# Norm chains of a two-block transformer kernel: filler products in PE's waits, a rounding without its lag, and earlier halves of two activation splits

## What is computed

```python
def modulate(x, shift, scale):
    return layer_norm(x) * (1 + scale) + shift
...
def mixer(p, kv, lw, rope):
    ...
    g_f, g_m, g_g = jnp.split(jax.nn.sigmoid(gate_logits + lw["b_gate"]), N_BRANCHES, axis=-1)
    return (g_f * y_f + g_m * y_m + g_g * y_g) @ lw["w_o"]

def sq_relu_mlp(h, lw):
    return jnp.square(jax.nn.relu(h @ lw["w1"])) @ lw["w2"]
...
        h_x = modulate(x, sh1, sc1)
        p_x = h_x @ lw["w_in"]
...
        x = layer_norm(alpha * x + g1 * mix_x, ln1_g[l], ln1_b[l])
        x = layer_norm(alpha * x + g2 * sq_relu_mlp(modulate(x, sh2, sc2), lw), ln2_g[l], ln2_b[l])
```

## Time and profile before

| | |
|---|---|
| median of 3 runs | 3077.68 us (3077.47 to 3078.82) |
| the profiled execution: its own time | 3078.22 us |
| its span, first to last instruction | 3076.0 us |
| mean granted TensorE clock | 0.959 of full speed |
| PE busy | 2901.8 us, 94% of the span |
| ACT, DVE, POOL busy | 1264.1, 963.1, 1813.2 us |

### The profile page before, as it was taken

How to read it: one execution, slowest core, us unless ns; L and a number is a source line. 1 busy time by engine, 2 the same in 40 slices (tenths; PEclk the granted TensorE clock), 3 DMA queues, 4 the chain that set the end, 5 groups by cost and what they waited for, 6 DMA issues and landing times.

```text
span 3076.0 us, 49253 instructions
## 1 busy us (share of the span) xinstructions
PE 2901.8 (94%) x20337; PEld 2573.1 (84%) x20337; DVE 963.1 (31%) x1757; ACT 1264.1 (41%) x1675; POOL 1813.2 (59%) x1380
## 2 busy tenths in 40 slices
PE   6989889999999998898999998999999999899999
PEld 4866658757878686797998998989999999889999
DVE  3133233232122334434144314144321314144331
ACT  2323533223222243644444435454444434455443
POOL 1310217414455240485895997747898997856896
PEclk8989989989999899998998999999999999999999
DMA  7325333212322234453553555534555556534553
GB/s 228 90 94 170 115 123 111 87 55 92 99 83 96 69 84 131 146 175 110 177 195 111 185 179 147 162 95 152 177 178 171 185 178 153 165 110 136 170 188 124
DMA packets 397419, 422.61 MB, mean 137 GB/s; under 512 B 74577, under 2 KB 367433, under 8 KB 396957
## 3 DMA queue, kind: packets, MB, share of 16 engines
q1 hardware_dynamic: 397246, 420.11, 44.1%
HBM read 419.01 MB, written 3.16 MB: 137 GB/s over the span
## 4 chain that ended last, share of the span: by engine, by line
PE 84%; POOL 5%; DVE 4%; ACT 2%; issue 2%; DMA 1%; SPq 1%; DVEq 0%; POOLq 0%; ACTq 0%
PE ps L830 64%; PE ps L814 18%; POOL ring_r L1637 5%; PE ps L857 2%; ACT ring_hi L1670 1%; DMA ring<-in_w_in 0%; DVE stat L2595 0%; SPq L596 0%; DVE arena_r L2818 0%; PE ps L1315 0%; DVE arena L2609 0%; DVE arena L2874 0%; SPq L562 0%; DVE arena L2568 0%; DMA ring<-in_ffn_w_up 0%
## 5 line engine op out<-in xcount | busy, mean ns | idle before, releaser
L1637 POOL TENSOR_TENSOR ring_r<-ring,ring_hi 128x512 fp32r<-128x512 f32 x1376 | 1813.0, 1355 | 1240.3 <-ACT ring_hi L1670 1239.9
L830 PE MATMUL ps<-hT_r,ring_hi 128*128 128x256 f32 (+1 forms) x6176 | 1148.2, 309 | 37.9 <-POOL ring_r L1637 23.8
L830 PEld LDWEIGHTS ps<-hT_r,ring_hi 128*128 128x128 f32 x6176 | 927.4, 195 | 111.5 <-issue 47.2
L1670 ACT ACTIVATE ring_hi<-ring 128x2048 fp32r<-128x2048 f32 x344 | 655.3, 1911 | 379.6 <-DMA ring<-in_ffn_w_down 110.3
L830 PE MATMUL ps<-hT_r,ring_r 128*128 128x256 f32 (+1 forms) x3088 | 695.7, 307 | 0.0
L830 PE MATMUL ps<-arena_r,ring_hi 128*128 128x256 f32 (+1 forms) x3536 | 598.7, 311 | 24.3 <-DVE arena_r L2684 10.1
L830 PEld LDWEIGHTS ps<-arena_r,ring_hi 128*128 128x128 f32 x3536 | 509.7, 193 | 63.6 <-issue 20.2
L830 PEld LDWEIGHTS ps<-hT_r,ring_r 128*128 128x128 f32 x3088 | 510.0, 195 | 24.2
L830 PE MATMUL ps<-arena_r,ring_r 128*128 128x256 f32 (+1 forms) x1768 | 334.4, 308 | 0.0
L830 PEld LDWEIGHTS ps<-arena_r,ring_r 128*128 128x128 f32 x1768 | 267.4, 192 | 16.1
L814 PE MATMUL ps<-arena 128*64 128x128 f32 (+9 forms) x1616 | 198.6, 362 | 26.3 <-DVE arena L2572 11.9
(11 more groups left out here) (295 smaller groups left out, 2376.0 us busy)
## 6 DMA issues: line engine op xcount, KB each, us to landing
ring<-in_w_in SPq DMA_DIRECT2D x82, 1024.0 KB
ring<-in_w SPq DMA_DIRECT2D x64, 1024.0 KB
ring<-in_w_ada SPq DMA_DIRECT2D x48, 1024.0 KB
ring<-in_ffn_w_up SPq DMA_DIRECT2D x44, 1024.0 KB
ring<-in_ffn_w_gate SPq DMA_DIRECT2D x44, 1024.0 KB
ring<-in_ffn_w_down SPq DMA_DIRECT2D x44, 1024.0 KB
ring<-in_w_in SPq DMA_DIRECT2D x48, 256.0 KB
ring<-in_w_o SPq DMA_DIRECT2D x8, 1024.0 KB
```

Source lines behind the costliest of these rows:

```text
L830: last[t] = pe.matmul(o, lhsT, rhs, start=start and j == 0, stop=stop and j == n - 1, skip_group_check=True)
L1637: ins = pool.tensor_tensor(k.ring_lo[s][:, part], k.ring[s][:, part], k.ring_hi[s][:, part], ALU.subtract)
L1670: act.activation(k.ring_hi[s][:, :], k.ring[s][:, :], ACT.Copy).then_inc(k.hi_ready[s], 1)
```

## The change

It makes five edits, all in the first block.

1. `awake(b, n)` issues n products of the identity with 256 columns of constants (plain float32, 128x128x256) into a bank that is about to be written anyway. In each of the four norm chains one stands before the statistics products, and four (two in the last chain) before the flip; nine stand before the first norm's panel.
2. In `coefficients` the `ends` flips move ahead of part 0, and part 1 behind the product with ones. Part 4 moves from before the first tile of h to after it.
3. `modulate_tokens` rounds each tile right behind its own L1715. DVE's low half follows two steps back instead of three. Where this norm is followed by two panels, one of ACT's `split` calls moves in behind tile 4, and is taken out further on.
4. The first half of the split of `mixed` (four tiles) moves into the last branch group: ACT's two roundings behind its sigmoids there, DVE's two subtractions ahead of its last four gated tiles.
5. The last round of up panels is unrolled. Hidden tiles 0 and 1 are rounded and subtracted ahead of the last two tiles' rectifying and squaring, and PE takes the down products of tile 0 bank by bank, each as its bank comes free.

```diff
+            def awake(b, n):
+
+                for _ in range(n):
+                    pe.matmul(ps[:, b, 0:256], ident, k.const[:, 0:256], start=True, stop=True, skip_group_check=True)
...
                 b = bank()
+                awake(b, 1)
                 pe.wait_ge(*k.moved(sums))
...
                 b = bank()
+                awake(b, 4 if tiles else 2)
                 pe.wait_ge(S["rows_ready"], T.next("rows_ready"))
...
-                part(0)
                 b = bank()
                 pe.wait_ge(S["rows_ready"], T.next("rows_ready"))
...
-                part(1)
+                part(0)
                 pe.wait_ge(*k.moved(ends))
                 T.again(b)
                 products(ps[:, b, 0:n], [(ones[0:1, :], token_ends[0:1, 0:n])]).then_inc(k.bank_done[b], 1)
+                part(1)
                 part(2)
...
                 part(3)
-                part(4)
                 w = view(panel(), 0, KD, 256)
                 for kt in range(KD):
-                    if 1 <= kt <= 3:
-                        part(kt + 4)
+                    if 1 <= kt <= 4:
+                        part(kt + 3)
...
+                    bs = [bank() for _ in range(2)]
+                    awake(bs[0], 9)
                     w = view(panel(), 0, KD, 256)
-                    bs = [bank() for _ in range(2)]
...
-                        bs = [bank() for _ in range(KD)]
-                        done = [(b, T.value(f"bank{b}")) for b in bs]
-                    mms = abreast([ps[:, b, 0:n] for b in bs],
-                                  [[(cut(w, ALL, kt % 2, slice(m * P, m * P + P)), x)] for m in range(KD)], kt == 0, False)
+                        bs, done, mms = [], [], []
+                        for m in range(KD):
+                            bs.append(bank())
+                            done.append(T.last())
+                            mms.append(products(ps[:, bs[m], 0:n], [(cut(w, ALL, 0, slice(m * P, m * P + P)), x)], True, False))
...
-                for kt in range(KD + 1):
...
+                    ins.then_inc(S["h_plain"], 1)
+                    act.wait_ge(S["h_plain"], T.next("h_plain"))
+                    act.activation(k.h[0][:, kt, cols], plain[:, kt, cols], ACT.Copy).then_inc(S["h_rounded"], 1)
+                    if kt == KD // 2 and last:
+                        split()
...
+                        if (c, g) == (1, 2):
+                            mixed_half(0, cols)
                         skip(4)
...
+                up(range(3))
+                split()
+                for kt in range(2):
+                    used = (T.bank + BANKS - 2 + kt) % BANKS
+                    act.wait_ge(k.bank_read[used], T.value(f"bank{used}"))
+                    rounded(kt)
+                for m in range(2):
+                    rectified(4 * KD - 2 + m, *T.take())
+                split()
...
-                for i in range(KD + 3):
+                for i in range(KD + 2):
...
-                    if i >= 3:
-                        low(i - 3)
+                    if i >= 2:
+                        low(i - 2)
...
+                        if (c, g) == (1, 2):
+                            mixed_low(0, cols)
                         for t in range(4):
...
+                for j in range(3 * KD, 4 * KD):
+                    if j == 4 * KD - 2:
+                        low(0)
+                        low(1)
+                    squared(j, hid[:, j, :])
```

More of the change, by code:

```diff
@@ L1794, in latent @@
                                    scale=k.vec(name, 2 * l + j)).then_inc(S["latent_rounded"], 1)
-                split()
+                if not behind:
+                    split()
                 for j in range(2):
@@ L1996, in mlp, with rounded @@
                     rectified(j, *T.take())
-                with act.Fori(0, 3) as i, T.loop(i, 3, {"panel": 4, "tiles": 8}):
-                    up()
-                act.wait_ge(*k.moved(T.last()))
-                for kt in range(4 * KD):
+                def rounded(kt):
+                    act.activation(hid_hi[:, kt % HID_SLOTS, :], hid[:, kt, :], ACT.Copy).then_inc(S["hid_rounded"], 1)
+                with act.Fori(0, 2) as i, T.loop(i, 2, {"panel": 4, "tiles": 8}):
+                    up()
+                up(range(3))
[6 more added lines that the diff above has]
+                    rectified(4 * KD - 2 + m, *T.take())
+                split()
+                for kt in range(2, 4 * KD):
                     if kt >= HID_SLOTS:
                         act.wait_ge(S["hid_used"], T.next("hid_used"))
-                    act.activation(hid_hi[:, kt % HID_SLOTS, :], hid[:, kt, :], ACT.Copy).then_inc(S["hid_rounded"], 1)
+                    else:
+                        used = (T.bank + BANKS - HID_SLOTS + kt) % BANKS
+                        act.wait_ge(k.bank_read[used], T.value(f"bank{used}"))
+                    rounded(kt)
                     if kt % 2 == 1:
@@ L2772, in _ @@
                         .then_inc(S["hid_split"], 1)
+                for j in range(3 * KD, 4 * KD):
[3 more added lines that the diff above has]
+                    squared(j, hid[:, j, :])
+                scratch = norm_scratch(cols, l == 1)
+                for kt in range(2, 4 * KD):
+                    if kt == 4:
+                        gain_powers("ln2", l, scratch)
+                    low(kt)
                 tiles = [T.take() for _ in range(KD)]
```

45 lines of the change are left out of this document (22 added, 23 removed).

## The result

The changed kernel takes 3053.69 us (median of 4 runs, 3050.42 to 3054.38) against 3078.25 of the kernel before (4 runs, 3077.47 to 3079.87): a ratio of 0.9917, 95% interval 0.9900 to 0.9935, so 24.6 us less. The profiled execution took 3053.52, its span 3051.7 (before 3076.0), at a mean granted clock of 0.966 (before 0.959). It lies 2.7 above the 3051 forecast, inside the range. By the spans the gain is 24.3: the places that the change touches gave 27.8, where the sum had 26.8, and places that it does not touch gave back 3.5.

The account below looks back on a forecast made before the run. PE was taken to bound the kernel, holding 84% of the chain, with time gained only where it stands still or runs at half clock. Terms of 26.8 us off 3078.22 gave 3051.4, forecast 3051, range 3033 to 3064.

Parts of the forecast that it names:

- the first norm: First norm's panel: earlier rounding and nine `awake` products let PE finish it sooner; 1.7 us gained, ends 0 and 2.9.
- the mixer's end of layer 0: PE's 5.30 us wait and the half clock behind it vanish through the split first half; 7.5 us, ends 6.5 and 7.8.
- ln1 of layer 0: Norm chain: first dense product at 673.7 instead of 677.72, less half clock; 2.3 us gained, 1.0 to 7.0.
- ln2 of layer 1: Layer 1's second norm chain: only `awake` products and order help; 0.8 us gained, ends 0 and 5.5.
- the wait behind ln1 of layer 1: PE's 1.84 us wait for POOL's low half, then half clock, shrinks through the moved `split`; 1.6 us, ends 0 and 3.5.
- ln1 of layer 1: Norm chain with 256 columns, 7.18 us at half clock behind its first dense product; 1.7 us gained, ends 0.5 and 5.
- The mixer's end of layer 1: Gated tiles 2.4 us later, PE 1.8 ahead, a clock fall may take all; 1.0 us gained, ends -1 and 3.
- B: Rival: the `awake` products hold full clock through the norm chains; 45.9 us gained, 3032 us; chance 0.15.
- C: Rival: the `awake` products do nothing for the clock; 20.6 us gained, 3057 us; chance 0.12.
- C2: Rival: DVE and POOL obstruct each other, taking about half the gains at mixer's ends and down starts; 3063 to 3065; chance 0.04.
- D: Rival: in layer 1's down, ACT's roundings behind panel landings make PE wait each panel; slower, 3111 us; chance 0.04.

Follow-up runs that it names:

- Halves alone: The kernel before with only the first half of the split of mixed moved into the last branch group: 3074.44 us, 0.9972 of the kernel before.
- down alone: The kernel before with only the down products begun among the last up tiles: 3078.57 us, 0.9989 of the kernel before.
- second profile: The changed kernel run once more, unaltered, on the chip of other experiments: 3053.77 us, 0.9908 of the kernel before.
- no fillers: The changed kernel without any `awake` product; order, rounding and both halves stay: 3069.52 us, 0.9961 of the kernel before.
- fillers alone: The kernel before with only the `awake` products added: 3070.22 us, 0.9968 of the kernel before.
- more fillers: The changed kernel with six more 128-row `awake` products in each of the three chains that feed two panels: 3059.35 us, 0.9931 of the kernel before.
- halves in layer 0 only: The changed kernel with the split of mixed in one piece again in layer 1: 3055.58 us, 0.9912 of the kernel before.
- thick parts: The changed kernel with each part over 128 rows: other operands, norms' shift left out, 3042.70 us; real rows with zeros under them, 3042.90 us, 0.9877.
- 3-row fillers: The changed kernel with `awake` products of a contraction of 3 rows instead of 128, same number and columns: 3067.11 us, 0.9953 of the kernel before.

## Why the prediction was right

**Right by its mechanism and its size:** the mixer's end of layer 0 (7.5 forecast, 7.5), the start of down in layer 0 (5.1, 5.3), ln2 of layer 0 (2.8, 3.1, of which up to 1.2 came without the edits), and the start of down in layer 1 (2.3, 2.5 at once, 1.7 to the end of the part). Halves alone and down alone gave the same steps in layer 0, so these terms add up as the sum took them to.

**Right in size here, less sure than it looks:** the first norm (1.7, 1.8). Its panel was read at 84.2 to 85.0 in eight profiles with fillers, at 85.62 without them, at 86.15 before; but at 87.98 and 89.55 in two more with fillers, and at 88.83 and 90.05 in two kernels with the code of before. These four had half clock over 17.1 us ahead of the norm, in one piece, where the others had it in two with full clock between; so 1 to 2 us are the edit's, among profiles that start alike, and 3 to 5 go with when the clock is down ahead of the norm. PE's timeline there, first of the changed kernel, then of its second profile:

```profile
54.61 4.16 PE L1326 MATMUL ps<-arena 33*128 33x8 f32 x30
```

```profile
55.18 6.57 PE L1326 MATMUL ps<-arena 33*128 33x8 f32 x30
```

**Right mechanism, wrong size:** ln1 of layer 0, the first dense product at 673.7 and 2.3 gained: measured 3.6. On the changed kernel's axis 673.7 is 666.0, and the product came at 665.16; the fall came at 661.40, during the parts, and the half clock behind the dense product was 3.14 us and not 5. A term of 1.6 was missing behind this chain. ln2 of layer 1: 0.8 forecast, 2.3; the new order alone gave 1.5 (no fillers), fillers alone 1.6.

**Right number, wrong reason:** the wait behind ln1 of layer 1 (1.6, 2.1). The prediction had it from the `split` moved in behind tile 4. The wait went from 1.84 to 1.27, that is by 0.6; but it did so also with fillers alone and with down alone, which do not move the `split`, and there too the step gained 2.1. In these two the chain ahead was 3.0 and 4.4 us slower, which gives POOL time as well, and a kernel without the moved `split` alone was not run. The other 1.5 is the fall of the clock behind the wait, which stayed away in these kernels. It came, with the `split` moved, in the kernels without fillers, with more fillers, with halves in layer 0 only and with thick parts, and there the step gained 0.6. So the term holds 0.6 that an edit can have given, and a fall that came or did not.

**Wrong:** ln1 of layer 1, 1.7 with ends 0.5 and 5: it lost 1.3, and in the second profile 2.5. The step that failed is that half clock behind the first dense product would be no longer than the 7.18 before, so that what the fillers put off would be gained. The fall did come later, 6.6 us into the chain and not 4.6, but the rise came 11.3 behind the first dense product. How long half clock lasts in this chain is not fixed by its code (13.7 and 23.9 us with the code of before), and what fixes it is open. The mixer's end of layer 1, 1.0 (gated tiles 2.4 later, PE 1.8 ahead less half a fall of the clock): the delay was 2.2, but the wait only went from 4.78 to 3.81, which is still long enough for that fall, 3.40 at half clock, and the step gained 0.2.

**Luck in the sum:** the terms came to 27.8 against 26.8, but by misses that cancel: 1.3, 1.6, 0.5 and 1.5 more in and behind the two ln1 chains and in ln2 of layer 1, 3.0, 0.8 and 0.6 less in ln1, the mixer's end and down of layer 1. Places that the change does not touch gave back 3.5 (1.65 lost in layer 0's attention, 0.97 gained in layer 1's, 2.84 lost in the second block). Part of that is the clock: in the second block half clock lasted 2.9 us longer in all, worth 1.5 of the 2.8; the rest was not traced. The changed kernel has stretches such as this one there, with PE busy throughout:

```profile
2334.00:2337.40 3.40, 3.40 (x18) 3.40 (x17) 0.65 (x2) 3.38 (x4) 0.90 (x1) 0.50 0.93 278
```

The kernel before had none there. Ten of the twelve experiments' profiles, halves alone and down alone among them, also took 1.0 to 8.4 us longer in the second block than the profile of the kernel before, so that profile was a short one there. In the other kernels the shift at the last result of layer 0's branches, before which only the first norm was edited, lay between -4.6 and +5.7. The stated ends of the terms add up to 13.5 and 49.1 and not to 13.7 and 48; the range does not hang on it.

**The rivals.** B (full clock throughout) did not happen with fillers, but its price was near: with thick parts the steps gained 4.6 to 6.7 in the chains, where B had 7.0, 7.0, 5.0 and 5.5. C (fillers do nothing) is out for ln1 of layer 0; a kernel without fillers gained 10.7 and not the 21 of C's sum, for the loss in layer 1's chain (5.7), the missing gains of ln1 in layer 0, and places without an edit. C2's mechanism shows in layer 1's mixer end alone. D is out: PE waits once at the end of layer 1's down part, before as after, for 3.0 to 6.5 us in these kernels, and not once a panel. The prediction put the roundings' lag and the parts' order under one head and never asked what one would do without the other: 42 us.

By the rule of the Trainium skill that activity releases the throttle (TensorE: Matmul & The Clock Gate, What's actually happening) a busy PE would have been enough; the fall among 3-row fillers at 653.40, PE busy 2.34 of 2.40 us before it and 1.80 of 1.80 behind it, speaks against that reading.

## What to carry to other kernels

A long gap on PE (3.39 to 5.30 us here) costs its length and then half of the stretch at 0.50 behind it, so closing a gap with real work, half of the next product's input made early, pays twice (7.5 for 5.3 idle). If the work in a chain is thin (few rows in the contraction), fill the rows with zeros rather than add more fillers: it costs a memset off the path and gave about 10 us here, on top of the fillers in the gaps (without those it was not run), where more fillers cost 6. And when PE's order and another engine's lag are changed together, write out for one tile which instruction of each engine waits for which; an edit that looks like latency alone may be what keeps a loop open.

## What the runs showed of the hardware

- The granted clock fell to 0.50 in the middle of back-to-back 3-row products with PE busy 2.34 of 2.40 us before the fall, and held at 1.00 over 12.85 us in which PE was busy 9.47, mostly with 128 rows. Rows of zeros counted like rows of data (3042.90 against 3042.70).
- With products of 256 columns and thin parts among them PE can stay at 0.50 for 27.3 us while 24.96 busy; with thick parts the same chain never left 1.00. With thin parts and one and the same code it was at 0.50 for 13.7 us in one profile and 23.9 in another.
- A part of 128 rows took no longer than one of 3 (1.02 against 1.12 for its two instructions at 512 columns and full clock).
- One DVE subtraction of 128x512 took 1.78 us beside POOL's L1648; two ran in 1.29 with POOL idle, 7 us later.
